# Feed-forward pairs: a fourth step with seven block products, and the residual added by transfers

## What is computed

```
u = _rmsnorm(h, norm_mlp_g)
a = jnp.einsum('bsd,df->bsf', u, w_up)        # 2048 -> 8192
a = jnp.square(jax.nn.relu(a))
h = h + jnp.einsum('bsf,fd->bsd', a, w_down)  # 8192 -> 2048
return _rmsnorm(h, norm_final_g)
```

## Time and profile before

| what | us |
|---|---|
| median of 3 runs (2112.61 to 2113.32) | 2112.98 |
| the profiled execution | 2112.74 |
| its span, first to last instruction | 2110.7 |
| PE busy in the span | 2090.6 (99%) |
| VectorE busy | 1446.0 (69%) |
| ScalarE busy | 1088.2 (52%) |
| GpSimd busy | 39.2 (2%) |

### The profile page before, as it was taken

How to read it: one execution, slowest core, us unless ns; L and a number is a source line. 1 busy time by engine, 2 the same in 40 slices (tenths; PEclk the granted TensorE clock), 3 DMA queues, 4 the chain that set the end, 5 groups by cost and what they waited for, 6 DMA issues and landing times.

```text
span 2110.7 us, 24975 instructions
## 1 busy us (share of the span) xinstructions
PE 2090.6 (99%) x10067; PEld 1754.5 (83%) x10067; DVE 1446.0 (69%) x1868; ACT 1088.2 (52%) x1409; POOL 39.2 (2%) x50
## 2 busy tenths in 40 slices
PE   8999999999999999999999999999999999999998
PEld 6888888888888888888888888888888888888886
DVE  5878788875555776556554455566896896797684
ACT  5545555555444675554445454354544554454453
POOL 0000000000000020000000000000000000000000
PEclk9999999999999999999999999999999999999999
DMA  7455555565465544365745542455555465556562
GB/s 270 181 182 197 200 186 213 182 243 193 172 218 198 189 147 171 125 235 199 294 179 181 191 167 100 160 200 185 196 204 193 168 231 185 185 189 219 182 218 98
DMA packets 56563, 402.60 MB, mean 191 GB/s; under 512 B 6240, under 2 KB 6496, under 8 KB 9216
## 3 DMA queue, kind: packets, MB, share of 16 engines
q1 hardware_dynamic: 53648, 380.67, 50.0%
q0 software_dynamic: 2656, 19.81, 2.4%
q10 hardware_dynamic: 144, 0.52, 0.1%
HBM read 392.59 MB, written 8.39 MB: 190 GB/s over the span
## 4 chain that ended last, share of the span: by engine, by line
PE 96%; ACT 1%; DVE 1%; issue 1%; DMA 0%; SPq 0%; POOLq 0%; POOL 0%; DVEq 0%; ACTq 0%
PE proj L617 15%; PE proj L619 15%; PE proj L618 15%; PE proj L1080 11%; PE proj L1083 6%; PE proj L722 4%; PE proj L723 4%; PE proj L724 4%; PE tbank L724 2%; PE tbank L723 2%; PE tbank L722 2%; PE tbank L576 2%; PE bank_a L722 1%; PE bank_a L724 1%; PE bank_a L723 1%; PE bank_b L724 1%
## 5 line engine op out<-in xcount | busy, mean ns | idle before, releaser
L1726 DVE TENSOR_TENSOR w_lo<-raw,w_hi 128x1024 fp32r<-128x1024 f32 x630 | 748.8, 1199 | 521.1 <-ACT w_hi L1186 513.9
L1186 ACT ACTIVATE w_hi<-raw 128x1024 fp32r<-128x1024 f32 x630 | 652.4, 1041 | 757.2 <-PE proj L619 480.8
L617 PE MATMUL proj<-w_hi,a_both 128*128 128x512 f32 x1280 | 513.3, 401 | 0.0
L619 PE MATMUL proj<-w_hi,a_both 128*128 128x512 f32 x1280 | 499.9, 391 | 0.0
L618 PE MATMUL proj<-w_lo,a_both 128*128 128x512 f32 x1280 | 498.4, 389 | 0.0
L619 PEld LDWEIGHTS proj<-w_hi,a_both 128*128 128x128 f32 x1280 | 240.2, 188 | 51.8
L618 PEld LDWEIGHTS proj<-w_lo,a_both 128*128 128x128 f32 x1280 | 240.7, 188 | 47.8
L617 PEld LDWEIGHTS proj<-w_hi,a_both 128*128 128x128 f32 x1280 | 240.6, 188 | 47.0
L1080 PE MATMUL proj<-a_both,w_hi 128*128 128x512 f32 x672 | 168.4, 392 | 0.3 <-DVE a_both L1772 0.3
L1080 PEld LDWEIGHTS proj<-a_both,w_hi 128*128 128x128 f32 x672 | 121.0, 189 | 22.2 <-DVE a_both L1772 0.5
L1186 ACT ACTIVATE w_hi_deep<-raw 128x1024 fp32r<-128x1024 f32 x84 | 85.7, 1025 | 94.1 <-PE proj L1083 57.6
(11 more groups left out here) (519 smaller groups left out, 3000.9 us busy)
## 6 DMA issues: line engine op xcount, KB each, us to landing
raw<-stream SPq DMA_DIRECT2D x359, 1024.0 KB, 4.8
nat<-x SPq DMA_DIRECT2D x4, 512.0 KB, 8.2
z_store<-z POOLq DMA_DIRECT2D x1, 2048.0 KB, 8.3
ga_store<-z POOLq DMA_DIRECT2D x1, 2048.0 KB, 12.3
gb_store<-z POOLq DMA_DIRECT2D x4, 512.0 KB, 7.2
yb<-z_store POOLq DMA_DIRECT2D x4, 512.0 KB, 10.0
ga<-ga_store POOLq DMA_DIRECT2D x1, 2048.0 KB, 8.0
gb<-gb_store POOLq DMA_DIRECT2D x1, 2048.0 KB, 14.5
```

What stands on the lines that cost most here:

```text
L617: nc.tensor.matmul(banks[t][:, :], ah, wh, start=first, stop=False)
L619: last = nc.tensor.matmul(banks[t][:, :], al, wh, start=False, stop=end)
L1186: A(hi_places[s][:, 0:width], src, ACT.Copy).then_inc(w_rounded, 1)
L1726: V.tensor_tensor(lo_places[s][:, 0:width], src, hi_places[s][:, 0:width].bitcast(f32), SUB).then_inc(w_rest, 1)
```

## The change

`SUM_AT` becomes (1, 2, 4, 5): one more step of each pair is done with seven products, and the place for the mixed banks' work moves from step 4 to step 6. The sums of mixed banks stay on VectorE, but nothing is added to `nat` by it. ScalarE writes each of the four mixed and four whole blocks, scaled, to one of four tiles `drain` (the halves of `stg` and `stg2`), and POOL adds each tile to its block of `nat` by a transfer with an add (`accum_op`). A tile is used twice in a pair, so the copy of a whole block waits until the mixed block's transfer has landed (`mixed_in`), and the next use of the tiles waits for `whole_in`. `part_read` counts one for VectorE's last read of a mixed bank and four for ScalarE's copies of the whole banks. Some tiles move to other places; the last sums' tiles are now single ones.

```diff
-SUM_AT = (1, 2, 3)
+SUM_AT = (1, 2, 4, 5)
...
+        drain = {2: stg2[:, 0, :], 3: stg[:, 1, :], 0: stg[:, 0, :], 1: stg2[:, 1, :]}
...
-            pool.wait_ge(w_rest, FIRST_PIECE[SUM_UNITS[-1]] + 4)
-            pool.dma_start(fg[:, :], fg_in).then_inc(fg_in_s, 16)
+            for q in range(PAIRS):
+                if q == PAIRS - 1:
+                    pool.wait_ge(w_rest, FIRST_PIECE[SUM_UNITS[-1]] + 4)
+                    pool.dma_start(fg[:, :], fg_in).then_inc(fg_in_s, 16)
+                n1 = 2 * (q % 2)
+                out_of = lambda o: nat[:, o // 2, (n1 + o % 2) * CW:(n1 + o % 2 + 1) * CW]
+                for i, (o, buf) in enumerate(((0, 2), (1, 3), (2, 0), (3, 1))):
+                    pool.wait_ge(mixed_scaled, 4 * q + i + 1)
+                    pool.dma_start(out_of(o), drain[buf], accum_op=ADD).then_inc(mixed_in[o], 16)
+                for i, o in enumerate(END_ORDER):
+                    pool.wait_ge(part_read, 5 * (PAIRS_IN + q) + 2 + i)
+                    pool.wait_ge(mixed_in[o], 16 * (q + 1))
+                    pool.dma_start(out_of(o), drain[o], accum_op=ADD).then_inc(whole_in[o], 16)
...
+            def wait_drains(q, places):
+
+                for o in places:
+                    act.wait_ge(whole_in[o], 16 * q)
+
+            def drain_whole(q):
+
+                from_mixed = {2: 0, 3: 1, 0: 2, 1: 3}
+                for i, o in enumerate(END_ORDER):
+                    if i < 3:
+                        act.wait_ge(part_done, 3 * (PAIRS_IN + q) + i + 1)
+                    else:
+                        act.wait_ge(w_used, done.at(RING + 2))
+                    act.wait_ge(mixed_in[from_mixed[o]], 16 * (q + 1))
+                    A(drain[o], parts[q % 2][o][:, :], ACT.Copy, scale=inv3_sq[:, o // 2:o // 2 + 1]).then_inc(part_read, 1)
 
...
                         if step == SUM_AT[-1] + 1 and j == 0:
                             act.wait_ge(w_used, done.at(RING))
                             if q % 2:
-                                act.wait_ge(part_read, 5 * (PAIRS_IN + q - 1) + 1)
+                                wait_drains(q, (2, 0))
                             else:
                                 act.wait_ge(proj_read, chunk.at() * 2)
-                            A(stg[:, 0, :], parts[1 - q % 2][0][:, :], ACT.Copy).then_inc(m_copied, 1)
+                                act.wait_ge(m_rest, up.at(UP_CHUNKS))
+                            m = parts[1 - q % 2][0][:, :]
+                            A(drain[2], m, ACT.Copy, scale=inv3_sq[:, 0:1]).then_inc(mixed_scaled, 1)
+                            A(drain[0], m, ACT.Copy).then_inc(m_copied, 1)
+                        if step == SUM_AT[-1] + 1 and j == 1:
+                            act.wait_ge(mixed_summed, q + 1)
+                            A(drain[3], drain[3], ACT.Copy, scale=inv3_neg[:, 0:1]).then_inc(mixed_scaled, 1)
+                    if step == STEPS - 1:
+                        act.wait_ge(part_read, 5 * (PAIRS_IN + q) + 1)
+                        A(drain[0], drain[0], ACT.Copy, scale=inv3_neg[:, 1:2]).then_inc(mixed_scaled, 1)
+                        A(drain[1], drain[1], ACT.Copy, scale=inv3_sq[:, 1:2]).then_inc(mixed_scaled, 1)
+                        drain_whole(q)
                     pieces(4 if step in SUM_AT else 2, slot=slot)
...
-                            act.wait_ge(part_read, 5 * (PAIRS_IN + 2 * n))
+                            wait_drains(2 * n, range(4))
...
-                    act.wait_ge(part_read, 5 * (PAIRS_IN + PAIRS))
+                    wait_drains(PAIRS, range(4))
...
             def add_mixed(q, part):
 
-                mixed, n1 = parts[1 - q % 2], 2 * (q % 2)
-                out = lambda t, n: nat[:, t, (n1 + n) * CW:(n1 + n + 1) * CW]
-                u, w = stg[:, 0, :], stg[:, 1, :]
+                mixed = parts[1 - q % 2]
+                u = drain[0]
                 if part == 0:
                     dve.wait_ge(w_used, done.at(RING))
-                    wait(dve, part_read, 5 * (PAIRS_IN + q))
                     dve.wait_ge(m_copied, PAIRS_IN + q + 1)
-                    V.scalar_tensor_tensor(out(0, 0), u, inv3_sq[:, 0:1], out(0, 0), MUL, ADD).then_inc(dve_seq, 1)
-                    seq.add()
+                    if q % 2:
+                        dve.wait_ge(whole_in[3], 16 * q)
                     chain(V.tensor_tensor(u, mixed[2][:, :], u, ADD))
-                    chain(V.tensor_tensor(w, mixed[1][:, :], u, ADD))
+                    V.tensor_tensor(drain[3], mixed[1][:, :], u, ADD).then_inc(mixed_summed, 1)
                 if part == 1:
+                    dve.wait_ge(mixed_summed, q + 1)
+                    if q % 2:
+                        dve.wait_ge(whole_in[1], 16 * q)
                     chain(V.tensor_tensor(u, mixed[3][:, :], u, ADD))
-                    V.scalar_tensor_tensor(out(0, 1), w, inv3_neg[:, 0:1], out(0, 1), MUL, ADD).then_inc(dve_seq, 1)
-                    seq.add()
-                    chain(V.scalar_tensor_tensor(out(1, 0), u, inv3_neg[:, 1:2], out(1, 0), MUL, ADD))
-                if part == 2:
-                    V.tensor_tensor(w, mixed[1][:, :], u, ADD).then_inc(part_read, 1)
-                    dve.wait_ge(part_read, 5 * (PAIRS_IN + q) + 1)
-                    V.scalar_tensor_tensor(out(1, 1), w, inv3_sq[:, 1:2], out(1, 1), MUL, ADD).then_inc(dve_seq, 1)
-                    seq.add()
-
-            def add_whole(q):
-
-                whole, n1 = parts[q % 2], 2 * (q % 2)
-                dve.wait_ge(dve_seq, seq.at())
-                for i, o in enumerate(END_ORDER):
-                    t, n = o // 2, o % 2
-                    if i < 3:
-                        dve.wait_ge(part_done, 3 * (PAIRS_IN + q) + i + 1)
-                    else:
-                        dve.wait_ge(w_used, done.at(RING + 2))
-                    y = nat[:, t, (n1 + n) * CW:(n1 + n + 1) * CW]
-                    V.scalar_tensor_tensor(y, whole[o][:, :], inv3_sq[:, t:t + 1], y, MUL, ADD).then_inc(part_read, 1)
+                    V.tensor_tensor(drain[1], mixed[1][:, :], u, ADD).then_inc(part_read, 1)
 
             def pair(q):
                 for step in range(STEPS):
@@ -2430,10 +2455,6 @@
                             rest_of_hidden(UP_CHUNKS - 1)
                         if step == SUM_AT[-1] + 1:
                             add_mixed(q, j)
-                        if step == SUM_AT[-1] + 2 and j == 0:
-                            add_mixed(q, 2)
-                    if step == STEPS - 1:
-                        add_whole(q)
                     pieces(4 if step in SUM_AT else 2, slot=slot)
 
```

More of the change, by code:

```diff
@@ L243, in build @@
         w_lo_deep = place("w_lo_deep", [P, 2, PIECE], f32r, 152.25)
[L244 to L248, removed]
+        ms_at = [160.25 + 4 * i for i in range(3)] + [190.25]
+        ms_hi = [place(f"ms_hi{i}", [P, 4, P], f32r, ms_at[i]) for i in range(len(SUM_AT))]
+        ms_lo = [place(f"ms_lo{i}", [P, 4, P], f32r, ms_at[i] + 2) for i in range(len(SUM_AT))]
+        ms = place("ms", [P, 4, P], f32, 172.25)
+        w_sum = place("w_sum", [P, 2, 2 * PIECE], f32, 174.25)
+        fg = place("fg", [P, D], f32, 174.25)
         hi_places = [w_hi[:, i, :] for i in range(RING)] + [w_hi_deep[:, i, :] for i in range(2)]
@@ L443, in build @@
         whole_added = sem("whole_added")
+        mixed_summed = sem("mixed_summed")
+        mixed_scaled = sem("mixed_scaled")
+        mixed_in = [sem(f"mixed_in{o}") for o in range(4)]
+        whole_in = [sem(f"whole_in{o}") for o in range(4)]
         out_ready = sem("out_ready")
@@ L1128, in pair @@
                         i = SUM_AT.index(step)
-                        sum_step(2 * step, whole, mixed, m_hi, m_lo, ms_hi[:, i], ms_lo[:, i], sums.at(i + 1), i == 0,
+                        sum_step(2 * step, whole, mixed, m_hi, m_lo, ms_hi[i], ms_lo[i], sums.at(i + 1), i == 0,
                                  i == len(SUM_AT) - 1)
@@ L1635, in round_sums @@
                 act.wait_ge(ms_summed, ms_sums.at(i + 1))
-                A(ms_hi[:, i, :, :], ms[:, :, :], ACT.Copy).then_inc(ms_rounded, 1)
+                A(ms_hi[i][:, :, :], ms[:, :, :], ACT.Copy).then_inc(ms_rounded, 1)
+            def wait_drains(q, places):
[10 more added lines that the diff above has]
+                    A(drain[o], parts[q % 2][o][:, :], ACT.Copy, scale=inv3_sq[:, o // 2:o // 2 + 1]).then_inc(part_read, 1)
             def chunk_squares(c):
@@ L2386, in rest_of_sums @@
                 dve.wait_ge(ms_rounded, ms_sums.at(i + 1))
-                V.tensor_tensor(ms_lo[:, i, :, :], ms[:, :, :], ms_hi[:, i, :, :].bitcast(f32), SUB).then_inc(ms_rest, 1)
+                V.tensor_tensor(ms_lo[i][:, :, :], ms[:, :, :], ms_hi[i][:, :, :].bitcast(f32), SUB).then_inc(ms_rest, 1)
             def add_mixed(q, part):
-                mixed, n1 = parts[1 - q % 2], 2 * (q % 2)
-                out = lambda t, n: nat[:, t, (n1 + n) * CW:(n1 + n + 1) * CW]
-                u, w = stg[:, 0, :], stg[:, 1, :]
```

(1 more changed line is left out.)

## The result

The changed kernel takes **2157.21 us** (median of four runs, 2156.42 to 2160.39), the kernel before beside it 2113.07 (2112.61 to 2113.32): a ratio of 1.0212, with a 95% interval of 1.0200 to 1.0224. It is slower by 44 us, where 9 were forecast and 21 was the top of the range. The profiled execution has a span of 2155.4 us against 2110.7, 44.7 more.

What follows compares the result with a forecast made beforehand. PE's number of matmuls was taken as the bound. At L = 4.0, even pairs' 8.7 us plus odd pairs' 4.65, less 4.8 for saved matmuls, gave +8.6 us, 2121.6; the range was 2112.5 to 2134.

Steps and rivals of the forecast that it cites:

- the six hand-overs: Three passages from an even pair into an odd one, three from an odd pair into the up projection; PE forecast late.
- E: The time at which PE ends a pair; 1713.7 in the even pair counted for the forecast.
- The other 0.4 us a pair: Even pairs' hand-overs: VectorE needs 16.6 us to step 4's first summed piece, PE could be there sooner; 0.4 us more.
- L: Time from POOL's start of an adding transfer's issue to its landing; taken as 4.0 us, forecast case 2.9 to 5.3.
- L - 1.5: End of an even pair: PE late by max(1.8, L-1.5) us, 2.5 at L = 4.0.
- the summed piece that I had counted: The next pair's first summed piece after an even pair: rest ready at E+6.0+L, needed by PE at E+7.5.
- E + 3.7 + L: End of an even pair: when ScalarE's last copy of a whole bank ends, behind the last mixed block's landing.
- L - 2.45: End of an odd pair: PE starts the up projection late by max(1.1, L-2.45) us, 1.55 at L = 4.0.
- my sum: Even pairs' 8.7 us plus odd pairs' 4.65 less 4.8 of saved matmuls: +8.6 us at L = 4.0.
- Rival (1): Adding transfers land late, as the 512 KB store did; all six hand-overs wait for a landing: 2130 to 2141, 17%.
- (2): Rival at the pairs' ends: VectorE isn't late and landings are near 2.9 us; no change, 2112.7, 17%.
- (3): Rival: mixed sums end before E and two whole banks are emptied by then; PE keeps 4.8 us, 2108.2, 6%.

Runs made afterwards that it cites:

- The halved stream: The changed kernel with only half of each weight unit loaded in the feed-forward part: 2141.71 us in one run.
- the plain copy: The changed kernel with the add taken out of the transfers, so each copies its tile over its block: 2143.9 us in one run.
- the second kernel with sooner mixed blocks: The changed kernel with sum steps 1 to 4, last two mixed blocks issued in step 6, odd pairs' whole blocks in tiles of their own: 2132.95 us.
- three sum steps: The changed kernel with sum steps 1 to 3, adding transfers and ScalarE's copies kept: 2125.61 us, ratio 1.0059.
- other tiles: The changed kernel with the odd pairs' whole blocks written to used places of the hidden blocks: 2145.68 us in one run.
- the kernel without landing waits: The changed kernel with sum steps 1 to 4, last mixed blocks issued in step 6, whole blocks placed to avoid late landings: 2119.55 us, ratio 1.0033.

## Why the prediction was right or wrong

- **Direction and place: right.** PE waits at the six hand-overs and nowhere else in the pairs, released by the instructions named; the 21 matmuls are gone; the seventh pair costs nothing.
- **VectorE: right.** Its second read of the mixed banks was forecast at E + 1.7 and ended at 1729.62, E + 1.4; PE was late by 1.4 us three times, where 1.8 was forecast. The other 0.4 us a pair, at step 4, doesn't show among PE's waits.
- **The formulas in L: right.** L - 1.5 for an even pair with the measured 6.7 gives 5.2; the two gaps are 1.43 + 3.53 = 5.0. One detail was off: in step 1 PE waited for the whole banks to be emptied, before it got to the summed piece that I had counted; the last copy ends at E + 3.7 + L and step 1 would begin at E + 5.46, so the formula is L - 1.76, which gives 4.9. L - 2.45 for an odd pair with 8.0 gives 5.5; the gap is 5.36.
- **L itself: wrong, the step that failed.** "With several in a row beside the weight stream I take 4.0" was read off 2.9 and 5.3 by bytes. The mixed blocks' transfers land after 7.1 at the median, and those that decide in the second slab after 6.7 and 8.0. 3.2 to 3.4 holds only for one issued first in a quiet stretch. My own row at the high end, the 512 KB store at 7.2, was the near one: also on POOL's queue and beside the weight stream. I discounted it by bytes. The halved stream takes 1.9 us off L, the plain copy 1.1, and the other adding transfers of the group hold the engines as well. The estimate from the fit in the Trainium skill, DMA: Bandwidth & Descriptors, section "Anatomy of one DMA", 3.2 with the issue, fits that one case and not the others.
- **The clock: left out.** Each gap was priced at its length, and the slow pace behind it at nothing. At L = 7.1 my sum is 3 x 6.0 + 3 x 4.65 - 4.8 = 27 us, 2140: 32 us of gaps, where 34.6 were measured. The slow pace adds 14.3. Rival (1), 2130 to 2141, was the nearest case and stopped short for the same reason.
- **Rivals (2) and (3): fell.** (2) needed VectorE in time and landings near 2.9, (3) the mixed banks read before E; they were read at E + 1.4, and L was 7.1.
- **A reading that was loose.** That none of the nine rows of waits is at a line of the pairs isn't so, as the row of `product` above shows; that PE waited for nothing in the feed-forward pairs is right.

## What to carry to other kernels

A buffer that is refilled only when an earlier transfer has landed puts that transfer's latency on the path, however idle the engines are: price it by the longest row with the same company on the DMA engines, not by its bytes, and count the other small transfers of its own group as company. Moving the issue earlier need not help, since it may move into heavier traffic; another place to write does, until the next user of that place waits. And price a gap on PE together with the pace behind it.

## What the runs showed that was not expected

- A 256 KB adding transfer inside SBUF took from 3.2 us to 9.8 in the changed kernel, and up to 14.9 in the second kernel with sooner mixed blocks; its issue took 0.85 us, against 0.54 without the add, and it held the 16 DMA engines for some 1.5 us, against 0.66.
- In the changed kernel the granted clock fell to 0.5 to 0.6 behind gaps of 3.5 us and more, six gaps with 14.3 us of slow pace together, and stayed at 1.00 behind the 1.4 us ones. In other runs it also fell behind single gaps of 1.9 us (to 0.57, three sum steps) and 2.6 us (to 0.50, other tiles). The Trainium skill, TensorE: Matmul & The Clock Gate, section "HAM oscillation — how this bites in real kernels", describes matmuls that start slow again after each wait for a DMA; the windows behind these gaps agree, those behind the 1.4 us ones don't show it. Matmuls by zeros in the gaps kept the pace.

## Left open

How the excess of L divides between the stream, the add and the other transfers of the group, and between sharing and order among the DMA engines, isn't itemised by these runs. In the kernel without landing waits (profiled at 2118.12) idle time is 7.1 us more than before and 3.2 us of busy time go beyond its matmuls, at a mean clock of 0.999; what those 3.2 us are stays open.
